# Input rows of an expert stage moved from GpSimd's queue into SyncE's queue of weight tiles

## What is computed

```python
def _expert_dispatch(xf, experts, weights, w_gate, w_up, w_down):
    ...
    def expert_block(args):
        tok, e = args
        xb = x_pad[tok]
        hb = jax.nn.silu(xb @ w_gate[e]) * (xb @ w_up[e])
        return hb @ w_down[e]
    yb = lax.map(expert_block, (buf_tok.reshape(n_blocks, MOE_BLOCK), blk_e))
    ...
```

## Time and profile before

| | |
|---|---|
| median of 3 runs | 3006.6 us (3006.18 to 3009.43) |
| profiled execution, its own time | 3005.8 us |
| its span | 3004.2 us |
| TensorE busy | 2772.1 us, 92% of the span |
| moved by DMA | 609.38 MB, mean 203 GB/s |
| SP's queue (q1, descriptors made by hardware) | 529.08 MB |
| GpSimd's queue (q0, made by software) | 53.49 MB |
| ScalarE's queue (q10, made by hardware) | 24.16 MB |

### The profile page before, as it was taken

The page is one execution under the profiler, slowest core; times in us unless marked ns, Lnnn a source line. Parts: engine busy times, 40 slices in busy tenths (PEclk is TensorE's granted clock), DMA queues, the critical chain, the costliest instruction groups (busy, mean ns, idle before and its releaser), DMA issues. The chain is left out here.

```text
span 3004.2 us, 41006 instructions
## 1 busy us (share of the span) xinstructions
PE 2772.1 (92%) x16557; PEld 1429.2 (48%) x16558; DVE 1107.4 (37%) x2434; ACT 661.3 (22%) x1262; POOL 210.8 (7%) x300
## 2 busy tenths in 40 slices
PE   7999999999999998999989899877998999989998
PEld 4644555555643232334467744477655333322343
DVE  2585455553510000004455635566464100000053
ACT  3310355541110000003420224422211000000132
POOL 0000000000100000002000000044211000000020
PEclk9999999999999999999999999988998999999999
DMA  4000594003499999997020210000417999999931
GB/s 165 28 9 20 223 408 154 1 28 136 181 339 407 409 410 410 409 410 259 29 74 1 33 56 28 1 2 2 178 57 273 364 409 411 411 410 402 398 127 42
DMA packets 137047, 609.38 MB, mean 203 GB/s; under 512 B 25700, under 2 KB 32260, under 8 KB 120456
## 3 DMA queue, kind: packets, MB, share of 16 engines
q1 hardware_dynamic: 111848, 529.08, 44.9%
q0 software_dynamic: 15296, 53.49, 4.9%
q10 hardware_dynamic: 9712, 24.16, 2.2%
HBM read 503.80 MB, written 101.71 MB: 202 GB/s over the span
## 5 line engine op out<-in xcount | busy, mean ns | idle before, releaser
L2804 PE MATMUL acc<-xt,work 128*128 128x512 f32 x384 | 166.9, 593 | 0.0
L672 PE MATMUL acc<-h,xt 128*128 128x512 f32 x384 | 165.2, 592 | 0.0
L310 PE MATMUL scores<-xt 65*128 65x512 f32 (+7 forms) x384 | 146.0, 489 | 0.4 <-DVE xt L451 0.4
L1715 PE MATMUL pg<-place 128*32 128x512 f32 (+2 forms) x736 | 137.7, 594 | 3.0 <-issue 3.0
L457 DVE TENSOR_REDUCE nmax<-scores 128x1 f32<-128x256 f32 (+7 forms) x128 | 96.8, 756 | 74.0 <-PE scores L312 70.3
L672 PEld LDWEIGHTS acc<-h,xt 128*128 128x128 f32 x384 | 72.9, 190 | 91.1 <-issue 90.9
L1221 PE MATMUL acc<-place 128*128 128x512 f32 x256 | 112.7, 594 | 1.1 <-PEq L71 1.1
L2804 PEld LDWEIGHTS acc<-xt,work 128*128 128x128 f32 x384 | 72.0, 190 | 86.1 <-issue 86.1
L1715 PE MATMUL pu<-place 128*32 128x512 f32 (+2 forms) x768 | 112.2, 624 | 0.8 <-issue 0.8
L1810 DVE COPY place<-py 128x512 f32<-128x512 f32 x21 | 14.5, 692 | 225.7 <-PE py L1715 225.7
L1810 DVE COPY work<-py 128x512 f32<-128x512 f32 x21 | 14.5, 692 | 224.4 <-PE py L1715 224.4
(11 more groups left out here) (763 smaller groups left out, 5422.6 us busy)
## 6 DMA issues: line engine op xcount, KB each, us to landing
place<-in_moe_w_gate_dram SPq DMA_DIRECT2D x21, 2048.0 KB, 23.7
place<-in_moe_w_up_dram SPq DMA_DIRECT2D x20, 2048.0 KB, 25.6
slots_out<-zeros SPq DMA_DIRECT2D x4, 9216.0 KB, 63.0
place<-in_moe_w_down_dram SPq DMA_DIRECT2D x18, 2048.0 KB, 25.7
xt<-in_moe_w_up_dram SPq DMA_DIRECT2D x17, 2048.0 KB, 25.4
xt<-in_moe_w_gate_dram SPq DMA_DIRECT2D x16, 2048.0 KB, 23.4
xt<-in_moe_w_down_dram SPq DMA_DIRECT2D x15, 2048.0 KB, 27.3
s_t<-in_moe_w_up_dram SPq DMA_DIRECT2D x11, 2048.0 KB, 25.9
```

Of the source, the lines that this page charges most:

```text
L310: pe.matmul(bank(n, u)[:, a * SLAB:a * SLAB + w], qkt[0:kind(p).rows, p % 2, u, 0, i * P:(i + 1) * P], qkt[0:kind(p).rows, p % 2, u, 1, a ...
L672: last = pe.matmul(acc[:, n % 4, 0:width], xs[:, k, tile_of(i)], weights[:, k, cols], start=(k == 0), stop=(k == k_of - 1))
L1715: last = pe.matmul(out[part], lhs[:, k, part], weights_of(kind, q)[:, k, cols], start=(k == 0), stop=(k == k_last), skip_group_check=True)
L2804: last = pe.matmul(acc[:, n % 4, :], slabs[m // 4 % 2][:, k, (m % 4) * P:(m % 4 + 1) * P], xt[:, k, half * SLAB:(half + 1) * SLAB], start= ...
```

## The change

GpSimd no longer loads input rows. SP does: ahead of the first tile whose place waits for something of unit n, it issues the rows of unit n+2, after a wait until unit n has been turned. In the order of tiles this puts them behind the last tile that waits for the up product of unit n-1 (from unit n = 1 on), and the rows of unit 2 behind the two tiles that have no wait. The expert numbers are read from the table as before, once each.

```diff
             @block.sync
             def _(sp):
                 expert = {}
+                asked = 0
+
+                def expert_of(q):
+                    if q not in expert:
+                        expert[q] = q if q < FIXED else sp.value_load(r.table[0:1, 3, q:q + 1], min_val=0, max_val=EXPERTS - 1)
+                    return expert[q]
+
+                def rows_in(n):
+                    sp.wait_ge(x_turned, n - 1)
+                    for x in units[n]:
+                        sp.dma_start(xb[x.row:x.row + x.rows, n % 2],
+                                     c.slots_in[bass.ds(expert_of(x.q) * REGION + x.slot, x.rows), :]).then_inc(x_in[n % 2], 16)
+
                 for n in range(preloaded, len(tiles)):
                     kind, q = tiles[n]
-                    if q not in expert:
-                        expert[q] = q if q < FIXED else sp.value_load(r.table[0:1, 3, q:q + 1], min_val=0, max_val=EXPERTS - 1)
+                    expert_of(q)
                     before = [x for x in range(n) if places[x] == places[n]]
                     if before:
                         used, by = tiles[before[-1]][0], last_user[tiles[before[-1]]]
+                        while asked < min(by + 1, UNITS - 2):
+                            rows_in(asked + 2)
+                            asked += 1
                         sp.wait_ge((gated, upped, downed)[used], (2 if used == 2 else 1) * (by + 1))
                     sp.dma_start(ring[places[n]].rearrange("p (k n) -> p k n", k=KF if kind == 2 else KD),
                                  views[kind][expert[q]]).then_inc(tile_in[places[n]], 16)
+                while asked < UNITS - 2:
+                    rows_in(asked + 2)
+                    asked += 1
                 clear_used(sp)
                 last_expert.update(expert)
...
             @block.gpsimd
             def _(pool):
-                expert = {q: q for q in range(FIXED)}
-
-                def rows_in(n):
-                    for x in units[n]:
-                        if x.q not in expert:
-                            expert[x.q] = pool.value_load(r.table[0:1, 3, x.q:x.q + 1], min_val=0, max_val=EXPERTS - 1)
-                        pool.dma_start(xb[x.row:x.row + x.rows, n % 2], c.slots_in[bass.ds(expert[x.q] * REGION + x.slot, x.rows), :]).then_inc(x_in[n % 2], 16)
-
-                for n in range(UNITS - 2):
-                    pool.wait_ge(x_turned, n + 1)
-                    rows_in(n + 2)
                 for n in (UNITS - 3, UNITS - 2):
                     pool.wait_ge(y_out[n % 2], y_before[n % 2] + 16 * arrivals[n])
```

## The result

The changed kernel is slower. Its median is 3070.56 us (4 runs, 3065.16 to 3075.59); the kernel before took 3008.01 us beside it (4 runs, 3006.18 to 3009.62). The ratio is 1.0209, with a 95% interval of 1.0196 to 1.0222. The forecast was 2996.1 us with a range of 2985 to 3009, so it missed by 74 us and on the wrong side.

A forecast was written before the change was run, and what follows sets the result against it. In the expert stages the bytes through the DMA engines set the pace; 32 groups x 0.61 = 19.6 us, less 32 x 0.28 = 9.1, gives 10.5 us, so 3006.6 - 10.5 = 2996.1 us, range 2985 to 3009.

The forecast's parts named there:

- the loss in the kernel before: Saturated part of both expert stages: input rows beside weights cost 19.6 us in all, 0.61 us per group.
- What loss stays?: Rows in SP's queue: 0.28 us per group stays of 0.61, so 10.5 us are saved over 32 groups.
- a second stream: Input rows on GpSimd's queue run beside the weights on the DMA engines; moving them to SP's queue removes this.
- the group 2420.5 to 2426: Stretch of layer 1 with rows among 4 KB packets only: 387 GB/s, loss 0.28 us, taken as nearest to SP's queue.
- nothing stays: Lower end of the loss left in SP's queue: consecutive tiles there follow one another at 408 GB/s or more.
- all 0.61 stays: Upper case for the loss left in SP's queue: all 0.61 us per group, or more.
- Rival 1: Nothing changes: the loss belongs to row pieces of 32, 64 and 96 partitions, wherever queued; 3006.6 us, 27%.
- Rival 3: Slower: rows in one queue stop all 16 DMA engines, next tile starts badly; 1.08 us per group, 3022 us; 11%.
- the warning: Near layer 1's start, rows among gate and up tiles ran at 282 GB/s; read as agreeing with the port rule, not proof.

The follow-up runs named there:

- one-transfer runs: Each unit's 128 rows in one transfer: changed kernel so altered (SP's queue) 2987.99 us; kernel before so altered (GpSimd's queue) 2984.28 us.
- the 16 spread ones: Changed kernel with rows in transfers of 16 rows, each to every eighth partition: 3082.96 us; with everything computed 3077.12 us.

## Why the prediction was wrong

**Right.** Both stages are bound by the DMA engines: a rate 5 to 7% lower gave 61 us, all of it seen at the end of the span. The issues on SP and the wait for the turn cost nothing (1.6 us in two waits), the rows came in time, and queue 0 gave up the 20 MB. The size of the loss in the kernel before was right as well: 19.6 us in 32 groups, where taking it away gave 22 us.

**The step that failed** is the one headed "What loss stays?". It took 0.28 us per group as the residual in SP's queue, on the premise that the loss was that of a second stream. Against whole transfers it measured 85.7/32 = 2.7 us, and against the kernel before the change cost 61.1/32 = 1.9 us per group where I had it save 0.33. Two choices made it. The first was the source of the loss. The 19.6 us came from comparing stretches with rows to stretches without; that says what rows in such a form cost, and nothing about the second queue. I put it down to the stream because a group among 4 KB packets lost less than one among 16 KB ones. The one-transfer runs show the loss to be that of the pieces: it vanishes on either queue when the transfer has 128 rows. The second was the neighbour: the group 2420.5 to 2426 ran in a second stream among 4 KB packets, and I carried its price into the weight queue, where "nothing stays" was my lower end and "all 0.61 stays" the nearest upper one. The price of a piece depends on the queue, 0.7, 1.3 and 2.7 us, and SP's is the highest.

The trace of the kernel before could already have refused the second choice. Of its 32 stretches with rows, 26 have at most a dozen packets over 8 KB, and by the sum of the prediction they lose 0.26 to 0.82 us, 0.56 on average; the six others lose 0.49 to 1.26, 0.83 on average. The 0.28 was the second lowest of the 32. This stretch has no larger packet at all and loses 5.5 x (1 - 358/408) = 0.67 us:

```profile
2523.50:2529.00 5.50, 5.50 (x56) 1.56 (x52) 0.69 (x1) 0.00 (x0) 0.00 (x0) 1.00 1.03 358
...
DMA packets 560, 1.97 MB, mean 358 GB/s; under 512 B 79, under 2 KB 79, under 8 KB 560
```

With 0.56 in place of 0.28 the forecast would have been a gain of under 2 us: closer, but still of the wrong sign, since no row showed the price in SP's queue.

**The rivals.** Rival 1 had the right cause, pieces of fewer than 128 partitions wherever queued, and missed that their price is not the same wherever queued. Rival 3 had the right sign and nearly the right picture, a tile behind the rows that moves badly, at 1.08 us. That its 231 GB/s is near the 259 measured is luck: the loads ahead of that stretch write all 128 partitions, and the share of 0.85 shows engines that idle, not slow packets. The length, 7 us against 2.5, it had too short. It explained the loss by all engines stopping together; whole transfers in the same place do not do this, so the place in the queue is not the mechanism. In hindsight was the warning: the rate with pieces of 64 rows in flight was already 282 GB/s. I set it aside because the DMA engines have time there; the share of 1.05 in that row says they had not.

**The rules set against the forecast.** For whole transfers the trace agrees with the Trainium skill, "DMA: Bandwidth & Descriptors", section "Issuing engines are not separate DMA queues": 2984.3 us from GpSimd and 2988.0 from SP, 0.1% apart. For partial ones the issuing engine is worth more than the time of its issues: 3008, 3026 and 3071 us from three of them. The measurement decides. The Trainium skill, "SBUF — State Buffer", section "Door 1: The DMA port swizzle", says that narrow partition ranges reach only part of the ports; 365 GB/s for half the partitions against 417 for all agrees in direction. By its mapping 16 neighbouring partitions of a block reach four ports and the 16 spread ones eight, so by it alone the spread ones should do better, and they did worse (380 GB/s against 390).

**What stays open.** Shown is that a load into SBUF of fewer than 128 partitions per transfer slows what runs around it, and that queue, source, number of transfers and number of packets do not cause it, though the queue and the place in it change its price. Why it does is not shown: the trace does not tell which DMA engine a packet ran on. Nor is it shown why the weight queue suffers most, or why blocks of 16 rows (3052 us) do less harm than 64 and 64 (3085) or 96 and 32 (3071).

## What to carry to other kernels

Where the DMA engines are the bound, load SBUF in transfers that write all 128 partitions, above all in the queue that carries the main stream; where the rows come from several places, gather them with one indirect transfer. Before moving a transfer to another queue, compare rates with and without that transfer and ask whether its loss belongs to its form or to its queue: one run with the transfer made whole tells it. The share of busy DMA engines does not show this loss, since it stays at 1.01 to 1.02; the rate does.

## What the runs showed of the hardware that I had not expected

- The DMA engines can be fully busy at 259 GB/s with 4 KB packets (1.04 share, 253 ns each) and at 417 with packets of the same size (1.03), depending on how many partitions the row transfers among them write.
- The slowdown reaches beyond the partial transfers: around 0.52 MB of rows some 1.3 MB of full-width down tiles moved at the same 259 GB/s.
- Result rows that leave SBUF in pieces of 96 and 32 partitions show no such harm: every kernel here has them, and those with whole loads run at 417 to 421 GB/s. No run leaves them out.
- A gather with one row per partition, made by software, is as fast beside the weights as a plain transfer of 128 neighbouring rows: 420 GB/s both in layer 0.
